# A two-layer transformer block on one core: the first modulation in two halves of the features, and a new pace for routing and for the second tokens' attention

## The reference

```python
mod = (silu(c) @ w_mod + b_mod)[:, None, :]
sh1, sc1, gt1, sh2, sc2, gt2 = jnp.split(mod, 6, axis=-1)
h = rmsnorm(x, ln_mix_g) * (1 + sc1) + sh1
proj = h @ w_in                      # queries, keys, values, gates, convolution inputs
x = x + gt1 * (mixed @ w_out)        # attention and convolution, mixed
h2 = rmsnorm(x, ln_ffn_g) * (1 + sc2) + sh2
# peer: per token 8 heads x 16 experts
u = expert_u[ec]
act = gelu(einsum('cd,ced->ce', xc, u))
einsum('ce,ced->cd', gc * act, expert_v[ec])
```

## Time and profile before

| | |
|---|---|
| median of three runs | 1257.31 us |
| the profiled execution, its time | 1260.68 us |
| its span | 1258.9 us |
| TensorE busy | 1078.0 us (86%) |
| VectorE busy | 796.0 us (63%) |
| ScalarE busy | 456.8 us (36%) |
| bytes moved | 432.08 MB, 343 GB/s over the span |
| first gather issued, last gather issued | 182.58 us, 970.47 us |

### The profile page before, as it was taken

The page is one execution under the profiler, slowest core; times in us unless marked ns, Lnnn a source line. Parts: engine busy times, 40 slices in busy tenths (PEclk is TensorE's granted clock), DMA queues, the critical chain, the costliest instruction groups (busy, mean ns, idle before and its releaser), DMA issues.

```text
span 1258.9 us, 13841 instructions
## 1 busy us (share of the span) xinstructions
PE 1078.0 (86%) x5002; PEld 536.8 (43%) x5002; DVE 796.0 (63%) x1865; ACT 456.8 (36%) x1257; POOL 295.8 (23%) x261
## 2 busy tenths in 40 slices
PE   6998986977887676769988789968998998999998
PEld 2887572432343222313332344423443444565543
DVE  5567758887763999764457667576655477645201
ACT  1132127555342444443353343434334423332201
POOL 0000013434343344433323333332323000000000
PEclk9999987998898889989999899988999999999999
DMA  9987419999999999999999999999999975344573
GB/s 388 409 328 316 169 47 370 364 354 411 421 383 421 417 404 395 378 423 401 421 421 420 421 421 420 420 422 363 421 420 423 380 268 200 142 160 154 212 293 127
DMA packets 63487, 432.08 MB, mean 343 GB/s; under 512 B 6931, under 2 KB 10300, under 8 KB 11836
## 3 DMA queue, kind: packets, MB, share of 16 engines
q0 software_dynamic: 36864, 268.45, 52.4%
q1 hardware_dynamic: 26160, 161.76, 32.3%
q10 hardware_dynamic: 396, 0.99, 0.2%
HBM read 430.12 MB, written 1.06 MB: 343 GB/s over the span
## 4 chain that ended last, share of the span: by engine, by line
PE 51%; DVE 20%; DMA 19%; ACT 5%; issue 2%; POOL 1%; another core or an unknown queue 0%; SPq 0%; DVEq 0%
PE ps L1140 22%; DMA AR<-in_puv,idx 17%; PE ps L1095 10%; DVE AR L1722 7%; PE ps L771 4%; PE ps L1254 3%; PE ps L990 2%; DMA W<-in_w_mod 2%; PE ps L1121 1%; PE ps L806 1%; POOL AR L2513 1%; PE ps L1035 1%; ACT av L2258 1%; DVE RT L1694 1%; ACT acc L2137 1%
## 5 line engine op out<-in xcount | busy, mean ns | idle before, releaser
L2513 POOL DMA_INDIRECT AR<-in_puv,idx x256 | 295.5, 1154 | 675.4 <-PE ps L1095 433.1
L1095 PE MATMUL ps<-AR,acc 128*64 128x512 f32 x904 | 286.6, 672 | 100.2 <-ACT acc L2137 98.4
L1722 DVE CUSTOM_DVE_ANT_0 AR<-AR,mixT 128x1024 f32<-128x1024 f32 x128 | 153.5, 1222 | 69.6 <-DMA AR<-in_puv,idx 69.3
L1140 PE MATMUL ps<-W,AR 128*128 128x512 f32 x416 | 189.2, 598 | 0.7 <-ACT AR L2137 0.7
L1095 PEld LDWEIGHTS ps<-AR,acc 128*64 128x64 f32 x904 | 71.8, 146 | 263.8 <-ACT acc L2137 169.5
L1722 DVE CUSTOM_DVE_ANT_0 AR<-AR,tok 128x1024 f32<-128x1024 f32 x128 | 153.0, 1220 | 48.4 <-DMA AR<-in_puv,idx 48.3
L1140 PE MATMUL ps<-W,hT 128*128 128x512 f32 x320 | 158.4, 626 | 6.5 <-DVE PT L2029 5.2
L2256 ACT ACTIVATE av<-av 128x1 f32<-128x1 f32 x256 | 51.3, 200 | 286.7 <-DVE av L1722 286.1
L1140 PEld LDWEIGHTS ps<-W,AR 128*128 128x128 f32 x416 | 76.1, 191 | 78.8 <-issue 76.7
L1140 PEld LDWEIGHTS ps<-W,hT 128*128 128x128 f32 x320 | 58.1, 198 | 83.3 <-issue 74.7
L2137 ACT ACTIVATE acc<-fold,av 128x64 f32<-128x64 f32 x226 | 78.6, 348 | 7.4
(11 more groups left out here) (459 smaller groups left out, 1311.2 us busy)
## 6 DMA issues: line engine op xcount, KB each, us to landing
W<-in_w_in SPq DMA_DIRECT2D x90, 1024.0 KB, 11.5
W<-in_w_mod SPq DMA_DIRECT2D x24, 1024.0 KB, 16.0
W<-in_wba SPq DMA_DIRECT2D x8, 1024.0 KB
W<-in_wbb SPq DMA_DIRECT2D x8, 1024.0 KB
W<-in_wo SPq DMA_DIRECT2D x8, 1024.0 KB
W<-in_w_out SPq DMA_DIRECT2D x4, 1024.0 KB, 5.7
W<-in_wq SPq DMA_DIRECT2D x4, 1024.0 KB
AR<-in_puv,idx POOLq DMA_INDIRECT x256
```

Of the source, the lines that this page charges most:

```text
L1095: t = mm(of(("E", a, c))[64 * g:64 * g + 64, :], dg_at((2 * p + g) % NDG, late), GB[:, places[g], D + c * 512:D + c * 512 + 512], start=(m ...
L1140: t = mm(b[:, :], src[:, k, :], slab(i)[:, k, :], start=(k == 0), stop=(k == 7))
L1722: ttr(GB[:, n, 0:D], GB[:, n, 0:D], H2[a][g], 1.0, 0.0, MUL, ADD, av[:, a, c:c + 1]).then_inc(*ve.sig("dot", p, g))
L2513: eng.indirect_dma_start(GB[:, n, :], None, puv, bass.IndirectOffsetOnAxis(ap=idx[:, a, c:c + 1], axis=0)).then_inc(*gp.dma(f"g{n}", "gat" ...
```

## The change

The slabs of shift and scale are loaded in the order "shift and scale of features 0 to 511, then of 512 to 1023", with half of the queries' slab between them. TensorE computes one-row products for the first two slabs only; VectorE computes all 512 columns of the other two. hT's first half is written when its own shift and scale are there, and queries and keys and values are then summed over features 0 to 511 before the second half is ready. Since several sums share a PSUM bank and stay open, the four banks are first opened by a product of 512 columns with zeros (`open_banks`). Slabs 4 and 9 get memory of their own. `mods(1)` and `mods(3)` move to later places on VectorE, and the loads of the slabs get another order and other waits. In the loop, three empty steps precede the attention of group 1, and the search of experts advances by 6 steps a turn until turn 16 and then by 4 (before: 6 until turn 7, 5 until turn 15, 4 until turn 32).

```diff
 
 SLABS = (
-    [("w_mod", n * 512, 512) for n in range(4)]
+    [("w_mod", n * 512, 512) for n in (0, 2, 1, 3)]
...
+SLOT = (0, 1, 2, 3, None, 1, 2, 0, 1, None, 0, 3, 0, 1, 2, 3, 0, 1, 2, 3, 0, 1)
+
+
 def slot_of(i):
-    return i % NSLOT if i < FRONT else RING[(i - FRONT) % 3]
+    return SLOT[i] if i < FRONT else RING[(i - FRONT) % 3]
 
...
+        for _ in range(3):
+            yield []
         yield [("scores_add", 4), ("gate2",)]
...
-        advance(routes, 6 if p < 8 else 5 if p < 16 else 4 if p < 33 else 8)
+        advance(routes, 6 if p < 17 else 4 if p < 33 else 8)
...
+        own = {S_Q: ar(12288, 4096).rearrange("p (k n) -> p k n", k=8), S_KW: ar(5952, 2240).rearrange("p (k n) -> p k n", k=8)}
+        MOD_AT = (0, 2, 1, 3)
+
         def slab(i):
-            return W[:, slot_of(i)]
+            return own[i] if i in own else W[:, slot_of(i)]
+
+        def quarters(v, part):
+
...
+            def mod_first():
+
+                take("modc")
+                open_banks()
+                for n in range(2):
...
+                mod_columns(0)
+                mod_columns(1).then_inc(*pe.sig("mod_cols", 0))
+
+            def mod_second():
+
+                mod_columns(2)
+                mod_columns(3).then_inc(*pe.sig("mod_cols", 1))
+                drop("modc", ("mod1", 1))
...
 
+            def open_banks():
+
+                for use in (("q", 0), ("q", 1), "c", "ksv"):
+                    b, old = take(use)
+                    pe.wait_ge(*old, "K", "zero")
+                    mm(b[:, :], ones[0:1, :], RT[0:1, 0:512], start=True, stop=False)
+
+            def queries_lo():
+                for j2 in range(2):
+                    for jj in range(2):
+                        feat(of(("q", j2)), jj * 256, S_Q, (2 * j2 + jj) * P, hT, h_k, k1=4, whole=False)
+
             def queries():
                 for j2 in range(2):
...
             bias_row()
-            mod_front()
-            norm_T("h", (0, 1), lambda a, k: tok2[:, a, k * P:k * P + P], lambda a: ("xb", a), h)
+            mod_first()
+            norm_T("h", (0, 1), x_at, lambda a: ("xb", a), h, k2s=range(3))
+            queries_lo()
+            norm_T("h", (0, 1), x_at, lambda a: ("xb", a), h, k2s=(3,))
+            keys_values_lo()
+            mod_second()
             queries()
...
 
             eng.memset(PT[32:33, 1, 0:8], NEG).then_inc(*ve.sig("neg"))
+            eng.memset(RT[0:1, 0:512], 0.0).then_inc(*ve.sig("zero"))
             ve.wait_ge("bias_mm")
             cp(fh, of("bias")[0:8, 0:383]).then_inc(*ve.sig("bias_row"))
             for a in range(2):
+                x_squares(a)
+            for a in range(2):
                 norm_x(a)
-            for n in range(4):
+            for n in range(2):
                 weighted_rows(n, half_buf(n)[:, 256:512], slice(256, 512), "mod_sum", n)
-            mod1()
-            evacuate("h", 0, S, sc1, sh1, ["mod1_sc"], h)
+            mod1(0)
+            evacuate("h", 0, S, sc1, sh1, [("mod1_sc", 0)], h, k2s=(0,))
+            for n in range(2, 4):
+                weighted_rows(n, half_buf(n), slice(0, 512), "mod_sum", n)
+            mod1(1)
+            evacuate("h", 0, S, sc1, sh1, [("mod1_sc", 1)], h, k2s=(2,))
             mods(0)
-            mods(1)
             blocks(0)
             blocks(1)
             flip_bias()
+            mods(1)
             mods(2)
-            mods(3)
             scores_add(0)
             weigh(0)
+            mods(3)
             scores_add(1)
...
             dma(X[:, :, :], x.rearrange("(a p) d -> p a d", p=P)).then_inc(*sp.dma("in_x", "x"))
-            for i in range(NSLOT):
-                load(i)
-            for i in range(NSLOT):
-                load(4 + i, ("modr", i), ("mod_sum", i))
+            load(0)
+            load(1)
+            load_part(S_Q, 0, "wq_lo", "wl", S_Q)
+            load(2)
+            load(3)
+            sp.wait_ge(("modr", 0), ("mod_sum", 0))
+            load_part(S_KV, 0, "wk_lo", "wl", S_KV)
+            load_part(S_Q, 4, "wq_hi", "w", S_Q)
+            load_part(S_KV, 4, "w0", "w", S_KV)
+            load(5, ("modr", 1), ("mod_sum", 1))
+            dma(cw[:, :], cmpw).then_inc(*sp.dma("in_cw", "cw"))
             sp.wait_ge("scr")
             dma(mixT[:, :, :], bass.AP(tensor=scr.tensor, offset=0, ap=[[1, P], [384, 8], [1, 256]])
                 ).then_inc(*sp.dma("in_skew", "skew"))
-            dma(cw[:, :], cmpw).then_inc(*sp.dma("in_cw", "cw"))
-            load(9, ("mods", 0))
-            load(10, ("mods", 1))
-            load(8, ("q_mm", 1))
-            load(11, "vs_mm")
-            load(13, "vw_mm")
-            load(12, ("mods", 2))
-            load(14, ("mods", 3))
+            load(S_KW)
+            load(11, ("mod_sum", 3))
+            load(6, ("mod_sum", 2))
+            load(8, ("mods", 0))
+            load(10, "ksv_mm")
+            load(14, ("mods", 1))
+            load(13, ("mods", 2))
+            load(12, ("mods", 3))
             load_row(2, ("rows", 2))
             dma(bdw[:, :, :], w_in2[:, 8 * 8192:8 * 8208].rearrange("p (k n) -> p k n", k=8)).then_inc(*sp.dma("in_bdw", "bdw"))
```

More of the change, by code:

```diff
@@ L56 @@
     "pe_vals": ("vn_mm", "S1_mm", "rest_mm", "ob_mm"),
-    "ve_cond": ("neg", "bias_row", "mod_sum", "mods", "mod1", "mod1_sc", "mod2", "mod2_sc", "g2c", "g1"),
+    "ve_cond": ("neg", "zero", "bias_row", "mod_sum", "mods", "mod1", "mod1_sc", "mod2", "mod2_sc", "g2c", "g1"),
     "ve_norm": ("x_sq", "xb", "n2_sq", "xn2"),
@@ L789, in bias_row, with mod_columns @@
                 mm(b[0:8, 0:383], tab, oh_sb, start=True, stop=True).then_inc(*pe.sig("bias_mm"))
[L791 to L800, removed]
-                for n in range(4):
+            def mod_columns(n):
+                cols, at = of("modc"), 4 * MOD_AT[n]
+                for j in range(4):
+                    c = slice(j * P, j * P + P)
+                    row = n < 2 and j < 2
+                    pe.wait_ge("K", ("mod_row", n) if row else ("mod_sum", n))
+                    lhsT, one = (half_buf(n)[0:1, c], ones[0:1, 0:1]) if row else (half_buf(n)[:, c], ones[:, 0:1])
+                    t = mm(cols[:, at + j:at + j + 1], lhsT, one, start=True, stop=True)
+                return t
+            def mod_first():
+                take("modc")
+                open_banks()
+                for n in range(2):
                     r, old = take(("modr", n), ("mod_row", n))
@@ L831, in keys_values, with keys_values_lo @@
+            def keys_values_lo():
+                for v in range(2):
+                    feat(of("c"), v * S, S_KV, v * P, hT, h_k, k1=4, whole=False)
+                feat(of("ksv"), 0, S_KV, 256, hT, h_k, k1=4, whole=False)
+                for a in range(2):
+                    token(of("ksv"), 256 + a * P, S_KV, 384, P, hT, a, h_k, k1=4, whole=False)
             def keys_values():
                 for v in range(2):
-                    b, old = take(("c", v), ("blk", v, 1))
-                    pe.wait_ge(*old)
@@ L835, in keys_values @@
[L835 to L840 removed]
+                    t = feat(of("c"), v * S, S_KV, v * P, hT, h_k, k0=4, whole=False, last=(v == 1))
+                t.then_inc(*pe.sig("c_mm"))
+                drop("c", ("blk", 0, 1), ("blk", 1, 1))
@@ L1432, in blocks @@
             def blocks(v):
[L1434 removed]
+                ve.wait_ge("c_mm", "cw")
                 for o in range(2):
@@ L2450, in scalar @@
                 x_root(a)
-            for n in range(4):
+            for n in range(2):
                 mod_row(n)
-            evacuate("h", (1, 3), 0, S, sc1, sh1, ["mod1_sc"], h)
+            for part in range(2):
+                evacuate("h", (1 + 2 * part,), 0, S, sc1, sh1, [("mod1_sc", part)], h)
             for j2 in range(2):
```

86 lines of the change are left out of this document (42 added, 44 removed).

## The result

The changed kernel has a median of 1262.74 us over 9 runs (1256.92 to 1269.17), against 1257.31 us for the kernel before in the same comparison. The ratio is 1.0051 with an interval of 1.0035 to 1.0068. The forecast was 1257.0, no change. So the change costs something between a fifth and half a per cent.

What follows compares the result with a forecast made beforehand. Transfers were taken to bound the long middle, so the first gather's time and lost transfer rate counted. 1260.7 + 4.8 - 5.1 = 1260.4 us profiled, 1257.0 on the median; range 1249 to 1265.

Steps and rivals of the forecast that it cites:

- The loop's term: Gather turns of the expert loop: two savings, -3.6 and -2.5 us, against +1 us; -5.1 us, between -9 and +3.
- the case of no change: Whole kernel: losses before the first gather and gains after it nearly cancel, 1254 to 1261 us; chance 0.38.
- the front's +4.8 us: Everything up to the first gather: issued 4.8 us later, near 187.4 us; between +2.1 and +6.3.
- the one-row products end at 26.0: TensorE at the start: openings and 32 products share one slow-clock stretch of 5.9 us, ending at 26.0 us.
- the 2.4 us that TensorE was to win: End of keys and values on TensorE: 61.6 us instead of 63.95, 2.4 us early.
- both waits for slabs: VectorE before the compressed keys and after: mods(4) waits 2.8 us; mods(6)'s earlier wait for slab 15, 5.96 us, carried over.
- second halves end 14 us after they begin: TensorE's second halves of queries, keys and values: begin at 47.6 us, end at 61.6.
- the relief of turns 0 to 2: First three loop turns: moving unit 4's attention out saves 2.5 us of the 18.9 us; bounds 0 and -3.8.
- the indices' wait: Turn 16's gather waits 6.32 us for VectorE's indices; the faster search removes it, -3.6 us, bounds 0 and -5.
- VectorE's denser search: Before turn 17: ten more search steps on VectorE, part of a +1 us cost, bounds 0 and +3.
- The slower one: Rival: mods(4)'s wait and mods(3) before unit 1 cost 6.3 us, the loop returns nothing; 1263.6 us, chance 0.28.
- The rival that halves overlap nothing: Queries end where they did, front +7 us or more, time near 1260 or above; within the 0.28 of The slower one.

Runs made afterwards that it cites:

- The front alone: The changed kernel with the old search pace put back and the three empty steps removed: 1267.24 us, ratio 1.008 to the kernel before.

## Why the prediction was wrong

**What held.** The places. mods(4) waits for a slab of w_mod near 100 us (3.73 us, 2.8 forecast), TensorE waits 9.95 us for the keys (9 forecast) and 1.24 us later (about 2), the clock's 1.5 us come back (1.6), and turn 16 no longer waits for its indices. The loop's term was -5.1 us, and -6.9 was measured, inside its bounds. The time, 1262.74 us, lies in the range of 1249 to 1265, but above the 1254 to 1261 of the case of no change.

**The step that failed is the front's +4.8 us, which had +6.3 as its upper end.** The front alone costs 9.6 us by the medians and 7.6 us in the profile. Three of its terms were too small. First, *the one-row products end at 26.0*: I let the openings' 512 columns share one slow start of 5.9 us with the products behind, so that they moved the end by 3.0 us (23.04 before). They kept the slow pace throughout (7.19 us), and the 32 products behind took 8.91 us all the same, inside the 8.64 to 9.89 of the old fronts. Nor was work begun earlier released earlier, as the forecast expected: the openings from 1.56 us on left those 32 products no faster. The end came at 28.3; against the same front with the openings early that is 6.2 us, and the 2.4 us that TensorE was to win shrank to 0.8. (The profile's granted clock reads 1.00 from the start of every trace, over these products too; that they ran slow, and the slow start in the forecast, are read from their durations alone.) Second, *both waits for slabs*: 3.73 for 2.8, and 7.48 for the 5.96 that I carried over from before, 2.4 us together. The second is 5.96 to 6.16 us in all four old fronts, and in the ten new ones 7.41 to 7.48 in seven and 6.02 to 6.08 in three; why it takes two values stays open. With the first term's 1.6 these are 4.0 us. Against them 1.0 us more came back at the end than I counted, which leaves 3.0 us, and the forecast 4.8 and the 7.6 of the profile are 2.8 apart. Third, not in the profile I had: the *second halves end 14 us after they begin*. In most executions they take 1.7 us more, because the clock falls behind the second one-column products, and VectorE has no slack to hide it. I had charged those products only their 2.2 us.

The Trainium skill (TensorE: Matmul & The Clock Gate, HAM oscillation) puts such falls down to idle gaps. The 32 products behind the 9.95 us wait, at 9.22 us instead of 7.07, agree with it (granted clock 0.50 up to 121 us). The fall behind the columns came with the gap filled by a one-row product, so TensorE need not be idle for it. The forecast had drawn about 10 us for the front from this rule, and 9.6 was measured, but that is luck: the slow work behind the keys still ended 1.24 us before VectorE's result, and the loss arose elsewhere.

**The loop** came out right partly for other reasons. Turn 3's first dot is 17.9 us behind turn 0's in after (195.83 to 213.69), where I wanted 17 and before had 18.9: the relief of turns 0 to 2 is 1.0 us, not 2.5. Turn 16 came 8.9 us nearer to turn 0, where the indices' wait was to give 3.6 and the first turns 2.5; some of that went to the new hole at turn 20, with VectorE busy 9.66 of 10 us. So the loop's sum was near and its terms were not. I had named VectorE's denser search as a cost of 1 us and the extra buffers that come three turns later, but had not seen a single place for them. My test "over 380 GB/s in the 115 us behind the first gather" failed (369), and no profile shows where the gain stands.

**The rivals.** The slower one was right on the sign and the place (slab 12's load behind mods(3)) and wrong on its condition: the loop did return its share, and the front cost more instead. That 1262.74 lies between its 1261 and 1263.6 is luck. The rival that halves overlap nothing came near: 0.8 us was all they won in that profile. It had the cause wrong: in that profile no product of queries, keys or values waited for a slab, and it was the openings that took the gain: with them out of the way keys and values ended at 60.20, 3.8 us sooner than before the change.

## What to carry to other kernels

When two halves of a stage are made to overlap, charge everything the split itself needs (openings, extra small products, their effect on the clock) to the engine that was to gain; here a saving forecast at 2.4 us ended as 0.8. Before work is moved on the engine that sets the path, follow the buffer that it frees, since the next load stands behind it. Measure the parts of a change apart: here one part was worth -6.9 us and the other +9.6, and the sum looked like nothing.

## What the runs showed of the hardware

- Eight one-row instructions of 512 columns take 7.19 us at the kernel's start, at 1.56 us as at 12.31 us. The 32 one-row products of 256 columns that follow are no faster for them: 8.83 to 10.02 us with them, 8.64 to 9.89 without.
- Behind one-column products over full tiles the granted clock was 0.50 in eight of ten profiled executions, with TensorE busy until a gap of 1.13 us, and with that gap filled as well. One one-row filler left the 32 products behind at 8.83 us; with two they took 9.99.
- The same load behind the same signal varies: in two executions of the changed kernel mods(6) waited 7.48 and 6.08 us for slab 15.
- Two executions of one kernel differed by 4.0 us at the end of the first projections (63.17 and 67.20 us), and four profiles of an unchanged front by 4.4 us at the first gather (179.76 to 184.15).
